# Ten reorderings in a Trainium2 kernel of three transformer blocks: weight splits, squares, a key unit, output chunks

## What is computed

```python
x = x + merged @ w_out          # block 1: rwkv7, stick-breaking and memory branches, gated and summed
x = x + conv_ffn(x, ...)
h = h + mlstm_mixer(h, ...)     # block 2
h = h + conv_ffn_2(h, ...)
h = h + moba_mixer(h, ...)      # block 3: attention with 8 heads
h = h + conv_ffn_2(h, ...)

def conv_ffn(x, norm_g, w_up, conv_w, conv_b, w_down):   # width 2 x 2816
    up = rms_norm(x, norm_g) @ w_up
    c = conv_b + sum of three taps of up, each shifted by one position, times conv_w[j]
    val, gate = halves of c
    return (silu(gate) * val) @ w_down
```

## Time and profile before

| | |
|---|---|
| Median of 3 runs | 1202.19 us (1202.01 to 1202.54) |
| The profiled execution | 1200.83 us |
| Its span, first to last instruction | 1198.8 us |
| Granted clock of PE, share of full speed | 0.999 |
| PE busy | 1161.2 us |
| DVE busy | 901.7 us |
| ACT busy | 662.6 us |
| POOL busy | 362.9 us |
| DMA | 188.77 MB, mean 157 GB/s |

### The profile page before, as it was taken

The page is one execution under the profiler, slowest core; times in us unless marked ns, Lnnn a source line. Parts: engine busy times, 40 slices in busy tenths (PEclk is TensorE's granted clock), DMA queues, the critical chain, the costliest instruction groups (busy, mean ns, idle before and its releaser), DMA issues.

```text
span 1198.8 us, 24765 instructions
## 1 busy us (share of the span) xinstructions
PE 1161.2 (97%) x9416; PEld 1074.1 (90%) x9416; DVE 901.7 (75%) x1305; ACT 662.6 (55%) x974; POOL 362.9 (30%) x326
## 2 busy tenths in 40 slices
PE   8999999899999999999999999999999989999998
PEld 8988678889999999989888999998898789999987
DVE  6989674456678888866757898887676768888853
ACT  5686943454445555544557565554455656555631
POOL 6634101000013555312102245550155023555400
PEclk9999999999999999999999999999999999999999
DMA  8644211236556555555432555555554325555551
GB/s 302 217 149 136 88 36 39 72 125 193 181 187 200 178 182 179 177 192 176 159 124 88 191 173 180 176 176 188 183 173 141 124 71 176 176 175 175 180 189 71
DMA packets 53987, 188.77 MB, mean 157 GB/s; under 512 B 6032, under 2 KB 6160, under 8 KB 53520
## 3 DMA queue, kind: packets, MB, share of 16 engines
q1 hardware_dynamic: 52304, 182.47, 46.9%
q10 hardware_dynamic: 1600, 5.12, 1.3%
HBM read 186.52 MB, written 1.05 MB: 156 GB/s over the span
## 4 chain that ended last, share of the span: by engine, by line
PE 78%; DVE 10%; ACT 7%; issue 3%; DMA 1%; POOL 0%; SPq 0%; DVEq 0%; ACTq 0%; POOLq 0%
PE psA L483 70%; PE psB L483 8%; ACT arena L1253 3%; DVE rounded L1878 3%; DVE arena L1881 3%; ACT rounded L1253 2%; DVE arena L1878 2%; ACT L1253 2%; DMA arena<-in_x 1%; DVE arena L2234 0%; DVE rounded L1881 0%; DVE arena L2389 0%; DVE arena L2330 0%; DVE arena L1912 0%; DVE arena L2283 0%
## 5 line engine op out<-in xcount | busy, mean ns | idle before, releaser
L483 PE MATMUL psA<-rounded,rounded 128*128 128x256 f32 (+1 forms) x7440 | 1011.6, 297 | 16.6 <-DVE rounded L1878 14.7
L483 PEld LDWEIGHTS psA<-rounded,rounded 128*128 128x128 f32 x7440 | 954.1, 191 | 67.3 <-issue 13.4
L1878 DVE TENSOR_TENSOR rounded<-arena,rounded 128x1024 fp32r<-128x1024 f32 (+2 forms) x362 | 458.4, 1287 | 71.6 <-ACT rounded L1253 67.8
L1253 ACT ACTIVATE rounded<-arena 128x1024 fp32r<-128x1024 f32 (+2 forms) x444 | 389.3, 922 | 184.3 <-PE psA L483 62.6
L1708 POOL TENSOR_TENSOR arena<-arena 128x256 f32<-128x256 f32 (+1 forms) x121 | 161.4, 1340 | 589.5 <-ACT arena L1253 220.9
L1253 ACT ACTIVATE arena<-arena 128x256 f32<-128x256 f32 (+6 forms) x276 | 145.4, 562 | 187.3 <-DVE arena L1878 135.1
L1881 DVE SCALAR_TENSOR_TENSOR arena<-arena 128x255 f32<-128x255 f32 (+4 forms) x338 | 177.5, 569 | 31.5 <-ACT arena L1253 21.3
L483 PE MATMUL psB<-arena 64*64 64x64 f32 (+9 forms) x1464 | 136.3, 285 | 10.1 <-DVE arena L1878 3.8
L483 PEld LDWEIGHTS psB<-arena 64*64 64x64 f32 (+4 forms) x1464 | 93.8, 152 | 41.8 <-issue 27.0
L1878 DVE TENSOR_TENSOR arena<-arena,psA 128x256 f32<-128x256 f32 (+1 forms) x84 | 38.4, 458 | 68.6 <-PE psA L483 43.4
L1795 POOL TENSOR_TENSOR rounded<-arena,rounded 128x256 f32 (+1 forms) x63 | 86.0, 1365 | 10.0 <-POOL rounded L1793 8.8
(11 more groups left out here) (73 smaller groups left out, 190.9 us busy)
## 6 DMA issues: line engine op xcount, KB each, us to landing
arena<-in_w SPq DMA_DIRECT2D x343, 512.0 KB, 3.5
arena<-in_mem ACTq DMA_DIRECT2D x2, 512.0 KB, 6.4
arena<-in_x ACTq DMA_DIRECT2D x1, 1024.0 KB, 4.9
arena<-in_con ACTq DMA_DIRECT2D x1, 1024.0 KB, 5.9
out<-arena SPq DMA_DIRECT2D x1, 1024.0 KB, 3.9
arena<-in_con ACTq DMA_DIRECT2D x1, 992.0 KB, 5.1
arena<-in_w SPq DMA_DIRECT2D x2, 256.0 KB, 3.2
arena<-in_x SPq DMA_DIRECT2D x2, 256.0 KB, 5.5
```

The source lines that it names most:

```text
L483: ins_ = nc.tensor.matmul(o, l, r, start=start, stop=stop, skip_group_check=shared)
L1253: return nc.scalar.activation(o, i, f, **kw)
L1878: return V.tensor_tensor(o, a, b, op)
```

## The change

Ten edits; all move or regroup work, and only the squares change engine.

1. ACT splits slots 1 and 2, then squares x in two operations of 128x1024 (`squares`), then splits on. POOL's part shrinks to `fold`: one sum of 128x1024 and one of 128x512.
2. The same for mem: ACT squares its halves after its shifts 2 and 3, and POOL folds them after chunk 5 of `rest_of("h_x")`, before chunks 6 and 7. PE waits for a count of 4.
3. In the first stage ACT splits one slot sooner, and DVE splits slots 9 to 12 right after its shift and before the normalized chunks.
4. DVE splits slot 28 before the four bonus products, and slot 30 between parts 2 and 3 of `head_norm`.
5. PE does half of `mk1` before `sb_sums(0)` to `(3)`; slots 32 and 33 are split on ACT ahead of `soft_log(0)` and on DVE ahead of `soft(0)`.
6. In all three FFNs the first four units split up to one or two slots sooner.
7. In the residuals after `wo`, `aw`, `bo` DVE splits a third slot between the two chunks of units 0 to 2.
8. ACT splits one slot more after the upper part of `h_a`.
9. Attention: the second of the slots after `bv11` is split ahead of the heads, the third at head 6 instead of at head 1 (DVE) and before head 0 (ACT).
10. The output is stored in eight DMAs of one chunk, each when its chunk is done.

```diff
@@ -470,9 +470,10 @@
             slot(i, j)
-    ready(sp, "x_final", KD)
-    sp.dma_start(out, xT).then_inc(sem("stored"), 16)
-    sp.wait_ge(sem("stored"), 16)
+    for k in range(KD):
+        ready(sp, "x_final", k + 1)
+        sp.dma_start(out[:, k, :], xT[:, k, :]).then_inc(sem("stored"), 16)
+    sp.wait_ge(sem("stored"), 16 * KD)
@@ -616,7 +617,7 @@
         o = open_(name)
-        ready(pe, f"sq_{tag}", 7)
+        ready(pe, f"sq_{tag}", 4 if tag in ("x", "m") else 7)
         for k in range(2):
@@ -740,9 +741,9 @@
     reduce_pairs(["bon0", "bon1"], bones, BN, "bonus_in")
+    project_mem("mk1", False, 0)
     for h in range(4):
         sb_sums(h)
-    project_mem("mk1", False, 0)
     project_mem("mk1", False, 1)
@@ -1293,6 +1294,13 @@
         A(fr(xgH[:, k, :]), xT[:, k, :], ACT.Copy, scale=pcol("n1", k)).then_inc(sem("xg_upper"), 1)
+    def squares(tag, dst, src, n):
+        c = slice(4 * n, 4 * n + 4)
+        A(dst[:, c, :], src, ACT.Square).then_inc(sem(f"sq_{tag}"), 1)
+    split_to(3)
+    for n in range(2):
+        squares("x", sqx, xT[:, 4 * n:4 * n + 4, :], n)
     split_to(6)
@@ -1313,8 +1321,11 @@
     for u in range(7):
-        split_to(min(SLOT_END[f"rw{u}"] + 4, 16))
+        split_to(min(SLOT_END[f"rw{u}"] + 5, 16))
         shift_own(u)
+        if u in (2, 3):
+            act.wait_ge(sem(f"ld_mem{u - 2}"), 16)
+            squares("m", sq1, mem_half[u - 2], u - 2)
         for k in H_AT[u - 1] if u else ():
@@ -1371,16 +1382,13 @@
     copy2("mq1", mqk[:, 2:4, :])
+    split_to(SLOT_END["mq1"] + 4)
         step(A(eb[:, hs, :], zb[:, hs, :], ACT.Abs))
-        if f:
-            split_to(SLOT_END["mq1"] + 3)
         step(A(eb[:, hs, :], eb[:, hs, :], ACT.Exp, scale=-1.0))
-        if f:
-            split_to(SLOT_END["mq1"] + 4)
         A(eb[:, hs, :], eb[:, hs, :], ACT.Ln, bias=1.0).then_inc(sem("sb_ln"), 1)
@@ -1533,11 +1541,13 @@
             act.wait_ge(*freed(f"up{f}.{j}"))
+            if j == 0:
+                split_to(s0 + 6)
             for m in range(2):
                     .then_inc(sem("tap2"), 1)
-            split_to(s0 + 2 * j + 6)
+            split_to(s0 + min(2 * j + 7, 12))
             ready(act, "conv", j + (f * UPS + 1))
@@ -1658,6 +1668,7 @@
     upper_of("h_a", HL, HH, KD, k0=4)
+    split_to(SLOT_END["bq0"] + 6)
@@ -1672,7 +1683,7 @@
     copies(["bv00", "bv01"], [av[:, t, 0:512] for t in range(TT)])
-    split_to(SLOT_END["bv11"] + 1)
+    split_to(SLOT_END["bv11"] + 2)
@@ -1687,8 +1698,9 @@
     copies(["bv10", "bv11"], [av[:, t, 512:1024] for t in range(TT)])
-    split_to(SLOT_END["bv11"] + 3)
     for h in range(9):
+        if h == 6:
+            split_to(SLOT_END["bv11"] + 3)
         if h < 8:
@@ -1722,15 +1734,17 @@
                 .then_inc(sem(f"sq_{tag}"), 1)
-    for n in range(len(X_AT)):
-        pool.wait_ge(sem(f"ld_x{n}"), 16)
-    ready(pool, "xg", KD)
-    for u in range(4):
-        square("x", sqx, xT[:, 2 * u:2 * u + 2, :], u)
-    for u in range(4):
-        pool.wait_ge(sem(f"ld_mem{u // 2}"), 16)
-        square("m", sq1, mem_half[u // 2][:, 2 * u % 4:2 * u % 4 + 2, :], u)
-    rest_of("h_x", HL, HH, "h_x")
+    def fold(tag, dst):
+        for n in range(2):
+            ready(pool, f"sq_{tag}", n + 2)
+            c, d = slice(0, 4 >> n), slice(4 >> n, 8 >> n)
+            nc.gpsimd.tensor_tensor(dst[:, c, :], dst[:, c, :], dst[:, d, :], ALU.add)\
+                .then_inc(sem(f"sq_{tag}"), 1)
+    fold("x", sqx)
+    rest_of("h_x", HL, HH, "h_x", 6)
+    fold("m", sq1)
+    rest_of("h_x", HL, HH, "h_x", KD, k0=6)
     pool.wait_ge(sem("ld_con"), 32)
@@ -1935,6 +1949,7 @@
         shifted(u)
+        split_to(min(10 + u, 14))
         for k in H_AT[u]:
@@ -1987,9 +2002,9 @@
     tt(LC, KM, LC, ALU.mult).then_inc(sem("fm"), 1)
+    split_to(29)
     for c in range(4):
         mark(stt(BN[:, c, :], r_[:, c, :], pcol("rk", c), KM[:, c, :], ALU.mult, ALU.mult))
-    split_to(29)
     settle()
@@ -1997,6 +2012,8 @@
         for u in range(4):
+            if u == 2:
+                split_to(SLOT_END["mq1"] + 1)
             c = slice(2 * u, 2 * u + 2)
@@ -2207,6 +2224,8 @@
                 for k in (2 * u, 2 * u + 1):
+                    if k % 2 and u < 3:
+                        split_to(SLOT_END[name] + 3)
                     ready(dve, f"xg_{tag}_upper", k + 1)
@@ -2237,12 +2256,11 @@
                     f"up{f}.{j}")
-            if j:
-                split_to(s0 + 2 * j + 4)
+            split_to(s0 + min(2 * j + 6 - j // 2, 11))
             ready(dve, "tap2", j * 2 + (f * UPS * 2 + 2))
             V.memset(small[:, 127:128], 0.0).then_inc(sem("conv"), 1)
-            split_to(s0 + 2 * j + 5)
+            split_to(s0 + (6, 8, 10, 11)[j])
@@ -2441,7 +2459,7 @@
             a_max(h + 2)
-        if h == 1:
+        if h == 6:
             split_to(SLOT_END["bv11"] + 3)
```

## The result

The changed kernel takes 1207.35 us (median of 6 runs, 1205.8 to 1208.73); the kernel before takes 1202.1 in runs beside it (6 runs, 1201.07 to 1202.93). The ratio is 1.0045, 95% interval 1.0035 to 1.0055: it is **slower by 5.2 us** where 6.2 faster was forecast. The profiled execution took 1207.37, its span is 1205.0 and its mean granted clock 0.997; before these were 1200.83, 1198.8 and 0.999.

A forecast was written before the change was run, and what follows sets the result against it. PE was taken as the bound, with only 37.6 us idle to win. Terms 0.6 - 1.1 + 0.2 + 4.2 + 1.0 + 0 + 1.3 = 6.2 off 1200.83 gave 1194.6, with 1.36 for the median 1196.0; range 1190.8 to 1199.5.

The forecast's parts named there:

- 4.2 gained: FFNs: earlier splits remove PE's waits at s0+5 and s0+6, 1.4 us in each of three FFNs.
- The forecast's lower end: FFNs: gain of 0 if DVE's whole lead is used up in the loop.
- rival C: FFN loops: DVE is the next bound, the 4.2 gain is lost again, 1200.2 us; chance 0.13.
- 0.2 gained: Stick-breaking: old waits go, the first scores wait 3.0, PE reaches sb_sums(4) 0.2 us earlier; ends 2.5 gained, 1 lost.
- All is given back: 0: Attention: 2.6 us of removed waits lost again before turn(7) through DVE's split at head 6; ends 2.6 gained, 1 lost.
- The 0.6 of edit 1: Slot 1: its split gets 0.6 us shorter with x squared on ACT and POOL quiet.
- the 1.1 lost: Slots 9 to 13 and mem's norm: 2.7 gained, then late fold; net 1.1 us lost, ends 2.7 gained, 2.5 lost.
- the 2.6 taken as the middle: Output store: a last store of 2.6 us, where the one store took 3.9; 1.3 us gained.
- Rival E: Fold of mem: chunk 5's rest ends after 60, PE stands 9 us more at rm, 1205.0 us; chance 0.05.

The follow-up runs named there:

- e1: The changed kernel with the earlier splits in all three FFNs undone on ACT and DVE; 1202.94 us, ratio 1.0004 to the kernel before.
- e6: The changed kernel with DVE's third split after bv11 at head 3 instead of head 6; 1204.66 us, ratio 1.0025 to the kernel before.
- e13: The kernel before with only the earlier FFN splits, plus DVE waiting for POOL's cast in one loop unit of four; 1211.65 us.
- e4: The changed kernel with slot 30's split moved back behind the four parts of head_norm; 1206.03 us, ratio 1.0036 to the kernel before.
- e7: The kernel before with only the store in eight DMAs added; 1199.77 us, ratio 0.9979.
- e5: The changed kernel with PE multiplying constant ones in its three long waits, 28 products; 1204.65 us, ratio 1.0021 to the kernel before.

## Why the prediction was wrong

**Edit 6** is the step that failed: "PE waits 0.18 and 0.90 ... 4.2 gained". The mechanism at the start was right, both waits went. What was wrong is the argument that let the gain last, that PE runs 144 records, six slots, without a wait behind 381.86. The row is read rightly: its matmuls start 0.120 apart, PE's own pace. But it is a lead being used up. Ahead of its scalings DVE was idle 0.80, 0.64 and then 0.0 us (387.89, 393.65, 399.41), the row ends in a wait of 0.16 at 399.53, and behind it a unit takes 5.86 to 5.90 and not 5.76, in delays too short to show as idle time. With edit 6 PE comes to these slots 1.6 earlier and DVE has no time in hand to follow: 1.6 gained, 1.8 to 1.9 lost again by s0+12. The forecast's lower end (0, and rival C, "DVE ... is the next bound in the loop") was this much of the truth. The other part, 2.4 in the second and the third FFN, was in no rival: the loop has two orders, and in the slower DVE's split begins ahead of POOL's cast; idle time of DVE under 0.17 us ahead of a scaling goes with it. Term: 4.2 gained, 4.7 lost in the trace (stages of the table); that is 8.9 of the 12.4 by which the span missed (6.2 less was forecast, 6.2 more came).

**Edits 4 and 5**: the wait before the first scores was forecast as 3.0 and was 3.33, and neither of the old waits at 106.19 and 125.36 came back. The stage lost 1.5 where 0.2 gained was forecast. The missing term is the clock, which halved behind the wait, 1.4 by the trace. e1's trace, with the same wait and no fall, has 0.0 for the stage, so the rest of this sum came out right to 0.2.

**Edit 9**: turn(2)'s wait went, the last turn waited 2.61 as forecast in kind ("in the attention one large wait, before the last turn"). "All is given back: 0" was 1.5 lost, 1.3 of it by the clock again.

**Edits 1 to 3**: 0.5 lost was forecast and 0.5 measured, which is luck in part. Slots 1, 9 and 10 gained 3.3, as forecast. A wait of 0.69 at slot 12 stood in no term; the fold ended at 54.45 and not near 55.3; and slot 14 began at 56.50, 0.6 later than before and not 1.5. The 0.6 of edit 1 could not be added to the 1.1 lost: PE stands behind the fold either way, so the forecast's own steps give 1.1 to 1.5 lost. The 0.7 lost at 74.80, where DVE is late with a reading of PSUM, was in no term either. **Edit 8**: 1.0, as forecast. **Edit 10**: 1.3 forecast, 2.0 measured; the last chunk took 1.9, below the 2.6 taken as the middle and the 3.3 of the smallest lone read. **Edit 7**: nothing lasting; from 671 to 681 us PE has gained 0.3 to 0.4, and behind that it is gone.

Rival E had the right sign from the wrong place: the fold ended at 54.45, never near 60.

The Trainium skill, SBUF — State Buffer, section Who interferes with whom, adds to its lock rule that issue order decides which of the two engines blocks, and that a VectorE operation with at most one SBUF input, outside the two-port modes, does not contend. By that rule the cast that begins during the scaling (which reads PSUM) gets through and one that begins behind the split does not, and the traces agree: 0.40 against 1.2 or more. I cited the lock for the fold and did not ask it of the loop, where the same two engines meet 54 times.

## What to carry to other kernels

A row with no idle time does not show that an engine is free. Before a gain ahead of a loop is booked as lasting, take the time from unit to unit well inside the loop (here 5.90) and compare it with the engine's own pace (5.76); the first units behind a wait may run on a lead, as here, and show nothing. Where two engines share a lock in a loop, look which begins first and by how much; if it is by hundredths of a us, any change ahead of the loop can turn the order, and a short delay of the right engine can be worth more than it costs. A pause of 2 to 3 us on PE can cost about 1.4 more than itself, in some executions and not in others.

## What the runs showed of the hardware

- Who begins first: POOL's cast of 128x256 took 0.40 when it began 0.02 or more ahead of DVE's split, 1.22 to 1.48 when it began later; the split 1.42 and 1.22.
- The granted clock went to half for 3.41 us (twice for 6.83, in e6 and e13) behind waits of 3.33 and 2.61, and in other traces around pairs of short ones close together, 1.39 and 0.86 (e4), 1.48 and 1.01 (e7). The same waits also passed without a fall: 3.33 in e1, the pairs in the changed kernel. It did not fall in the profiled run in which the long pauses were filled with products (e5), though the 1.48 and 1.01 stand there too.
- Stores of 128 KB landed 1.9 us after their issue when they came 5 us or more apart (the last three), 3.4 to 3.9 when five were issued within 2 us; the one of 1024 KB took 3.9.
